# Order of the wide matmuls in the gate, up and down projections: tiles in pairs, two with the high weights, then two with the low ones

## The reference, cut to what matters

```python
D_MODEL, SEQ, D_FF = 2048, 256, 5632
x = x + concat(y_fox, y_ssd) @ w_out
h = rmsnorm(x, ffn_norm_w)
g, up = split(h @ w_gate_up, [D_FF])      # 2048 x 11264
g = causal_dwconv(g, ffn_conv_w, ffn_conv_b)
x = x + (silu(g) * up) @ w_down           # 5632 x 2048
```

## Time and profile before

| What | Value |
|---|---|
| Median of 3 runs | 1251.85 us (1251.77 to 1252.63) |
| The profiled execution | 1251.71 us |
| Its span, first to last instruction | 1250.0 us |
| TensorE matmul busy, share of the span | 99% |
| TensorE weight load busy | 89% |
| VectorE, ScalarE, GpSimd busy | 69%, 49%, 5% |
| Mean granted TensorE clock | 0.998 of full speed |
| Instructions in all | 21434 |

### The profile page before, as it was taken

One profiled execution on the slowest core, in us unless ns is written; L12 is line 12 of the kernel. 1 busy time (PEld: TensorE's weight loads), 2 busy tenths in 40 slices (PEclk: granted clock), 3 DMA queues, 4 the chain that ended last, 5 costly groups with the idle time before them and its releaser, 6 DMA issues.

```text
span 1250.0 us, 21434 instructions
## 1 busy us (share of the span) xinstructions
PE 1236.6 (99%) x7838; PEld 1108.1 (89%) x7838; DVE 857.1 (69%) x1122; ACT 616.9 (49%) x810; POOL 60.8 (5%) x66
## 2 busy tenths in 40 slices
PE   8999999999999999999999999999999999999997
PEld 7999998899999888888888888888888888888885
DVE  6699887777777867767677676766746464646554
ACT  6544665665544544444444444544434343444554
POOL 2000000001221100000000000000001010101000
PEclk9999999999999999999999999999999999999999
DMA  8566555445556566666666666666665656566652
GB/s 259 168 181 189 165 157 154 119 119 159 183 181 196 181 194 188 186 195 187 188 185 193 192 186 192 187 191 188 192 190 167 210 165 216 165 212 205 192 185 101
DMA packets 165884, 226.94 MB, mean 182 GB/s; under 512 B 10208, under 2 KB 101380, under 8 KB 165700
## 3 DMA queue, kind: packets, MB, share of 16 engines
q1 hardware_dynamic: 165732, 225.90, 59.5%
q0 software_dynamic: 96, 0.26, 0.1%
HBM read 224.03 MB, written 2.10 MB: 181 GB/s over the span
## 4 chain that ended last, share of the span: by engine, by line
PE 97%; DVE 1%; DMA 1%; ACT 0%; SPq 0%; issue 0%; ACTq 0%; DVEq 0%
PE ps L344 39%; PE ps L346 20%; PE ps L332 8%; PE ps L333 8%; PE ps L334 8%; PE ps L372 4%; PE ps L374 4%; PE ps L373 4%; DMA w_raw<-in_w_in 1%; PE ps L807 1%; PE ps L763 1%; PE ps L820 0%; DVE h_parts L1242 0%; PE ps L790 0%; PE ps L777 0%; PE ps L805 0%
## 5 line engine op out<-in xcount | busy, mean ns | idle before, releaser
L317 DVE TENSOR_TENSOR w_lo<-w_raw,w_hi 128x1024 fp32r<-128x1024 f32 x413 | 505.6, 1229 | 317.0 <-ACT w_hi L312 316.0
L312 ACT ACTIVATE w_hi<-w_raw 128x1024 fp32r<-128x1024 f32 x413 | 435.8, 1059 | 455.6 <-PE ps L346 339.9
L344 PE MATMUL ps<-h_parts,w_hi 128*128 128x512 f32 x1408 | 488.6, 394 | 0.0
L346 PE MATMUL ps<-h_parts,w_lo 128*128 128x256 f32 x1408 | 390.2, 277 | 0.0
L344 PEld LDWEIGHTS ps<-h_parts,w_hi 128*128 128x128 f32 x1408 | 264.0, 188 | 61.7
L346 PEld LDWEIGHTS ps<-h_parts,w_lo 128*128 128x128 f32 x1408 | 264.1, 188 | 0.0
L344 PE MATMUL ps<-act_parts,w_hi 128*128 (+1 forms) x704 | 244.4, 392 | 0.0
L346 PE MATMUL ps<-act_parts,w_lo 128*128 (+1 forms) x704 | 196.8, 280 | 0.0
L332 PE MATMUL ps<-h_parts,w_hi 128*128 128x256 f32 x576 | 165.9, 288 | 0.9 <-DVE w_lo L317 0.9
L333 PE MATMUL ps<-h_parts,w_hi 128*128 128x256 f32 x576 | 162.9, 283 | 0.0
L334 PE MATMUL ps<-h_parts,w_lo 128*128 128x256 f32 x576 | 162.8, 283 | 0.0
(11 more groups left out here) (250 smaller groups left out, 1115.8 us busy)
## 6 DMA issues: line engine op xcount, KB each, us to landing
w_raw<-in_w_gate_up SPq DMA_DIRECT2D x352, 256.0 KB, 3.2
w_raw<-in_w_in SPq DMA_DIRECT2D x88, 512.0 KB, 3.7
w_raw<-in_w_down SPq DMA_DIRECT2D x88, 512.0 KB, 4.5
w_raw<-in_w_out SPq DMA_DIRECT2D x32, 512.0 KB, 4.6
w_raw<-in_w_ple_gate SPq DMA_DIRECT2D x32, 512.0 KB, 4.5
w_raw<-in_w_ple_proj SPq DMA_DIRECT2D x4, 512.0 KB, 5.3
out_x<-out_tok SPq DMA_DIRECT2D x8, 256.0 KB, 2.9
xtok<-in_x SPq DMA_DIRECT2D x3, 512.0 KB, 8.4
```

The source lines that it names most:

```text
L312: act.activation(parts(n)[0], w_raw[:, n % RING, :], ACT.Copy).then_inc(w_hi_made, 1)
L317: dve.tensor_tensor(lo, w_raw[:, n % RING, :], hi, ALU.subtract).then_inc(w_lo_made, 1)
L344: pe.matmul(ps[:, bank_of[m], :], hi, both.rearrange("p b t -> p (b t)"), start=first and k == 0, stop=False, skip_group_check=True)
L346: mm = pe.matmul(ps[:, bank_of[m], T:2 * T], lo, both[:, 0, :], start=False, stop=last and k == 1, skip_group_check=True)
```

## The change

For gate, up and down projection, the eight tiles of a chunk are taken in four pairs of neighbouring tiles (always with the same `k`, and with `m` = 0, 1 or 2, 3). For each pair the two 512-column matmuls with the high weights are issued first, then the two 256-column matmuls with the low weights. The order is thus 512, 512, 256, 256 where it was 512, 256, 512, 256. Operands, destinations, start and stop flags, the wait at the head and the count on the last matmul are the same; the expression for the activations is evaluated once for each matmul rather than once for each tile.

```diff
         def multiply_wide(pe, n, both_of, bank_of, first, last, q=0):
 
             pe.wait_ge(w_lo_made, n + RING * q + 1)
-            for i in range(2 * MT):
-                k, m = divmod(i, MT)
-                both = both_of(k)
-                hi, lo = (w[:, n % RING, i * P:(i + 1) * P] for w in (w_hi, w_lo))
-                pe.matmul(ps[:, bank_of[m], :], hi, both.rearrange("p b t -> p (b t)"),
-                          start=first and k == 0, stop=False, skip_group_check=True)
-                mm = pe.matmul(ps[:, bank_of[m], T:2 * T], lo, both[:, 0, :],
-                               start=False, stop=last and k == 1, skip_group_check=True)
+            for pair in range(MT):
+                tiles = [(i, *divmod(i, MT)) for i in (2 * pair, 2 * pair + 1)]
+                for i, k, m in tiles:
+                    pe.matmul(ps[:, bank_of[m], :], w_hi[:, n % RING, i * P:(i + 1) * P],
+                              both_of(k).rearrange("p b t -> p (b t)"), start=first and k == 0, stop=False, skip_group_check=True)
+                for i, k, m in tiles:
+                    mm = pe.matmul(ps[:, bank_of[m], T:2 * T], w_lo[:, n % RING, i * P:(i + 1) * P], both_of(k)[:, 0, :],
+                                   start=False, stop=last and k == 1, skip_group_check=True)
             return mm.then_inc(w_used, 1)
```

## The result

The changed kernel takes 1258.32 us in the median (1258.1 to 1261.35, 5 runs), the kernel before 1251.87 us beside it: a ratio of 1.0053 with a 95% interval of 1.0041 to 1.0064. That is 6.5 us slower, over the 0.2% from which a difference can be told here, and 1.8 us above the stated range. The profiled execution is the slowest of the five, 1261.35 us. The 3 us by which it stands over the others are most likely those ahead of the two stages: the gate stage starts at 406.8 us where it started at 403.7 in the kernel before, and the load of `xtok` takes 11.0 us to land where it took 8.4. The stages themselves are read from it.

A forecast was written before the change was run, and what follows sets the result against it. TensorE's own instruction pace was taken to bound the kernel. The profiled 1251.7 us less 0.5 us gave 1251.2; as that execution lies 0.1 us under the median, 1251.4 us was forecast, range 1244.0 to 1256.5 us.

The forecast's parts named there:

- The cost goes with the matmul, not with its neighbour: Gate and down stages: 226.7 + 120.0 = 346.7 ns for a tile in either order, against 347.1 measured.
- the sum: Gate and down stages: a pair of tiles takes 693.7 ns against 694.2, so -0.5 us over 1056 pairs.
- 226.7 + 234 + 120.0 + 113: Forecast ns for a pair's steps in both stages: 512-to-512, 512-to-256, 256-to-256, 256-to-512; 693.7 in all.
- same-bank rival: Gate and down stages: 256 waits 7 ns for its 512's bank; pairing removes it, -7.9 us, 1244.0 us; chance 0.12.
- rival of long pairs: Gate and down stages: 512-to-512 goes at 234.5 ns, 7.7 us slower, 1259.5 us; chance 0.12.
- rival on loads further ahead: Gate and down stages: weight loads brought in earlier, 256-to-256 falls to 110 ns, 10.6 us less, 1240.8 us; chance 0.05.
- the slower case: Gate and down stages: slow 512-to-512 0.12, part of it or an unseen stall 0.04; 0.16 in all, up to 1259.5 us.

The follow-up runs named there:

- g1_new_back: Changed kernel with 32 bytes of filling in SBUF behind the weight rings, just ahead of the arena: 1253.1 us, ratio 1.0013 to the kernel before.
- e1_other_bank: Kernel before, old order, but each 256-column matmul adds onto the PSUM bank of the other tile of its pair: 1253.1 us.
- e1_same_bank: Changed kernel, but both tiles of a pair write the same PSUM bank: 1259.2 us.
- e3_load_shift: Changed kernel, but weight loads read 32 bytes earlier in the chunk for seven tiles of eight, no tensor moved: 1256.7 us.
- e2_eights: Changed kernel with all eight 512-column matmuls of a chunk first, then all eight 256-column ones: 1258.1 us.
- f1_old_extra128: Kernel before plus two single 128-column matmuls, ahead of the gate stage's second unit and the down stage's first chunk: 1261.0 us.
- e3_new_both: Changed kernel with 32 bytes between h_parts and the weight rings and 32 more ahead of the arena: 1258.2 us, ratio 1.0055 to the kernel before.

## Why the prediction was wrong

**The step that failed** is the sentence "The cost goes with the matmul, not with its neighbour", with the sum built on it: -0.5 us was forecast, +6.5 came. The sum took one price for each kind of step from rows elsewhere, as if a kind of step had one price. It has several. In the terms of the sum, 226.7 + 234 + 120.0 + 113 was forecast for a pair; measured were 233 + 233 + 115 + 116 in the gate stage and 232 + 237 + 120 + 118 in the down stage. In the down stage of g1_new_back the same four steps were 226, 235, 118 and 113 in the median, within 2 ns of each term. So the terms were not wrong prices of the new order; they were the prices of one rhythm of several. 346.7 ns a tile, 226.7 + 120.0, is right for the fast rhythm, and both orders run in it (the new one in the down stage of g1_new_back). But the old order ran at 353.4 when a short matmul or two fillings met it badly, and the new order, at the addresses and with the history of this kernel, fell into 348.3 in the gate stage and 353.4 in the down stage. So the additive sum gave the floor, not the time, and the agreement of 346.7 with the stage's 347.1 was the agreement of two places that both happened to be near the floor.

**What the rows already showed.** 512-to-512 at 226.7 and at 234.5, 256-to-256 at 120.0 and 117.1: I took each for the price of a place, and the mean of 347.1 for one pace, where it holds 352 and 346.6. A step that has two prices in one trace, with equal shapes, says that something beside the shape sets it. The mixed steps have two prices too: 234 and 113 were read off a few rows, while over all starts 512-to-256 and 256-to-512 are 232 and 115 ns in the gate stage of the kernel before and 229 and 118 in its down stage. Their sum is 347 each time, so the forecast didn't suffer by it, but the 7 ns on which the same-bank rival was built are 5 and 3.

**The parts that held.** Nothing but TensorE's pace moved, no wait came in, and the register instructions stayed 128. The point on which the rival of long pairs was to decide, 512-to-512 above 229.6 ns, came true, with 233 and 232 ns, and its 1259.5 us is nearest to the 1258.3 measured. Its mechanism isn't what the runs show: in the gate stage the longer steps were mostly given back by 256-to-256 at 115 ns, in the down stage 512-to-512 was 5 ns over its term, but so was 256-to-512, with 3 ns more in 512-to-256, and 32 bytes took all of it away there. That its price was near is luck. The same-bank rival fell by e1_other_bank and e1_same_bank. Each of the 4224 loads of the two stages of the changed kernel starts beside the matmul just ahead of its own, so the rival on loads further ahead fell too.

**The range** reached to 1256.5 because I halved the slower case. Nothing in the rows told which of the two prices of 512-to-512 would hold, so the whole 1259.5 of that rival belonged inside.

The Trainium skill, in "TensorE: Matmul & The Clock Gate", section "Step-by-step: what each phase is for", says that TensorE has two independent read ports, so that loading the next tile takes no read bandwidth from the matmul that runs. Here a load that reads 32 bytes elsewhere, and nothing else, changed the pace from 353.4 to 348.6 ns a tile (e3_load_shift). The measurement decides: where a load reads can set the pace at which loads and matmuls follow each other, two ports or not. Whether they share bandwidth no run here shows.

**What stays open.** Which addresses and which history lead to which rhythm, and what in the engine holds it, wasn't found; addresses and history both act. Whether the new order can reach 346.7 ns in the gate stage is open as well: it ran at 348.3 with three widths of extra matmul and with the rings 1536 bytes further on, at 349.1 with the loads 32 bytes off and at 351.3 with two fillings. If it can't, about 2 us of the loss belong to the order there; the 4.3 us of the down stage don't.

## What to carry to other kernels

Where TensorE is bound by a stream of load-and-matmul pairs, read its pace in several windows, the first chunks and those behind each interruption too, and not as one mean: two paces for one loop body mean that an edit can move the stage by 2% either way without touching what it means to touch. Before an order, a layout or an inserted matmul is called better or worse by less than that, try it again with a filling of 32 bytes ahead of one operand; if the sign changes (here the old order won by 6.5 us on one layout and lost by 7.3 us on another), the rhythm was measured, not the edit. Once a layout is fixed, look whether the stage runs at its floor, and if it doesn't, try the cheap shifts first.

## What the runs showed of the hardware

The paces are few and sharp. In whole chunks of eight 512-column and eight 256-column matmuls, the values that came chunk after chunk were 2773, 2787, 2793, 2807, 2813 and 2827 ns (2807 in the first half of the down stage of e2_eights). Some rhythms repeat over several chunks instead: 2830, 2831 and 2819 ns in the gate stage of f1_old_extra128, 2827 on average, and averages of 2811 in the gate stage of e3_new_both and of 2816 in the second half of the down stage of e2_eights. To a tenth of a nanosecond the six steady values are 2773.3, 2786.7, 2793.3, 2806.7, 2813.3 and 2826.7 ns, or 832, 836, 838, 842, 844 and 848 cycles of 2.4 GHz for a tile: whole numbers, and even ones. At the granted full clock of 2.4 GHz the columns alone are 6144 / 2.4 = 2560 ns, so the fastest rhythm seen, called the floor here, has 13.3 ns on each of the 16 matmuls, and the slowest steady one 16.7. A rhythm can hold over 169 chunks, over loop turns and over changes of the ring's slot. Nearly all the changes seen came where TensorE was interrupted or its operands changed; in the changed kernel the pace went from 2787 to 2827 at the very chunk at which the down stage begins. The exception is e2_eights, which left 2807 ns after 48 chunks of the down stage, just where the kernel before pauses, but with no pause to be seen. An interruption need not change it: the down stage of the kernel before pauses twice, for 0.11 us each time, at 1025.6 and 1086.8 us, and comes back to 2773 ns both times. One matmul of 128 columns, put between two tiles, was enough to lose the fast rhythm for the 475 us that were left of the gate stage (f1_old_extra128).
